# Input projections of linear attention and recurrence: from full-precision products to three rounded passes, with ScalarE and GpSimd splitting the weights

## What is computed

```
proj = h @ w_in                      # attention: 1024 x 3088, q, k, v, g, a_lr
log_a = log_sigmoid(a_lr @ w_gate_up + b_gate) / 16
...
proj = h @ w_in                      # recurrence: 1024 x 2048
gate_br, xb = split(proj)
xc = causal depthwise conv(xb)       # 4 taps
r, i = sigmoid(xc @ w_r + b_r), sigmoid(xc @ w_i + b_i)
h = modulate(rmsnorm(x, gain), shift, scale)     # ahead of both
```

## Time and profile before

| | us |
|---|---|
| median of 3 runs | 1944.4 (1943.58 to 1946.43) |
| the profiled execution | 1949.44 |
| its span | 1947.6 |
| TensorE busy in it | 1828.3 (94%) |
| VectorE, ScalarE busy | 1056.6, 733.3 |
| mean granted TensorE clock | 0.966 of 2.4 GHz |
| attention's input, first low-rank product to the end of slot 11 | 34.7 to 155 |
| recurrence's input, first product to the end of slot 7 | 600.6 to 676.6 |

### The profile page before, as it was taken

How to read it: one execution, slowest core, us unless ns; L and a number is a source line. 1 busy time by engine, 2 the same in 40 slices (tenths; PEclk the granted TensorE clock), 3 DMA queues, 4 the chain that set the end, 5 groups by cost and what they waited for, 6 DMA issues and landing times.

```text
span 1947.6 us, 22802 instructions
## 1 busy us (share of the span) xinstructions
PE 1828.3 (94%) x9181; PEld 1409.1 (72%) x9181; DVE 1056.6 (54%) x1561; ACT 733.3 (38%) x944; POOL 0.2 (0%) x4
## 2 busy tenths in 40 slices
PE   6999999999998989999999989998798899989998
PEld 3786677767777756777677756766445767779998
DVE  1332644447884336544478744037923663438886
ACT  3212433334662415322446640126624333034443
POOL 0000000000000000000000000000000000000000
PEclk9999899998999998999999989999899999989999
DMA  9847666687984696577868902335422222345550
GB/s 360 266 136 260 236 238 259 260 324 259 365 319 136 198 320 258 197 277 285 333 244 333 341 22 87 108 109 194 130 65 65 87 87 87 110 148 176 193 174 23
DMA packets 178593, 392.92 MB, mean 202 GB/s; under 512 B 11317, under 2 KB 102056, under 8 KB 162104
## 3 DMA queue, kind: packets, MB, share of 16 engines
q1 hardware_dynamic: 176814, 389.58, 56.4%
q10 hardware_dynamic: 1674, 1.88, 0.3%
HBM read 390.39 MB, written 1.05 MB: 201 GB/s over the span
## 4 chain that ended last, share of the span: by engine, by line
PE 85%; DVE 8%; ACT 3%; DMA 2%; issue 1%; SPq 0%; DVEq 0%; ACTq 0%
PE bank L493 20%; PE bank L767 18%; PE bank L795 9%; PE bank L1193 7%; PE bank L503 4%; PE bank L598 4%; PE bank L1204 3%; PE bank L779 3%; PE bank L558 3%; DVE work L1728 2%; DMA ring<-in_ada_w_dram 2%; PE bank L1149 2%; PE bank L810 1%; PE bank L515 1%; DVE parts L1978 1%
## 5 line engine op out<-in xcount | busy, mean ns | idle before, releaser
L1978 DVE TENSOR_TENSOR parts<-ring,parts 128x2048 fp32r<-128x2048 f32 x144 | 329.1, 2290 | 168.4 <-ACT parts L1424 167.4
L767 PE MATMUL bank<-parts 128*128 128x512 f32 x1536 | 369.1, 399 | 8.0 <-issue 4.7
L493 PE MATMUL bank<-hh,ring 128*128 128x256 f32 (+1 forms) x1408 | 369.5, 422 | 6.1 <-ACT hh L1329 3.7
L1424 ACT ACTIVATE parts<-ring 128x2048 fp32r<-128x2048 f32 x144 | 275.2, 1917 | 228.6 <-PE bank L767 162.3
L767 PEld LDWEIGHTS bank<-parts 128*128 128x128 f32 x1536 | 292.5, 192 | 77.7 <-issue 17.0
L493 PEld LDWEIGHTS bank<-hh,ring 128*128 128x128 f32 x1408 | 268.6, 192 | 106.4 <-issue 76.4
L1286 ACT ACTIVATE work<-bank 128x256 f32<-128x256 f32 (+3 forms) x223 | 98.3, 445 | 518.2 <-PE bank L493 254.1
L795 PE MATMUL bank<-parts 128*128 128x512 f32 x768 | 179.4, 391 | 3.7 <-DVE parts L2003 3.7
L795 PEld LDWEIGHTS bank<-parts 128*128 128x128 f32 x768 | 143.4, 188 | 36.7 <-DVE parts L2003 4.1
L1193 PE MATMUL bank<-parts 128*128 128x256 f32 x1056 | 131.1, 287 | 7.6 <-DVE parts L2481 7.6
L1193 PEld LDWEIGHTS bank<-parts 128*128 128x128 f32 x1056 | 130.1, 196 | 8.4 <-DVE parts L2481 8.4
(11 more groups left out here) (273 smaller groups left out, 1779.9 us busy)
## 6 DMA issues: line engine op xcount, KB each, us to landing
ring<-in_moe_w_gate_dram SPq DMA_DIRECT2D x64, 1024.0 KB, 6.5
ring<-in_moe_w_up_dram SPq DMA_DIRECT2D x64, 1024.0 KB, 7.4
ring<-in_moe_w_down_dram SPq DMA_DIRECT2D x64, 1024.0 KB, 6.8
ring<-in_ada_w_dram SPq DMA_DIRECT2D x48, 1024.0 KB, 7.3
ring<-in_w_in_dram SPq DMA_DIRECT2D x32, 1024.0 KB, 5.9
ring<-in_w_mod_dram SPq DMA_DIRECT2D x24, 1024.0 KB, 5.7
ring<-in_w_up_dram SPq DMA_DIRECT2D x22, 1024.0 KB, 5.1
ring<-in_gla_w_in_dram SPq DMA_DIRECT2D x12, 1024.0 KB, 7.7
```

Of the source, the lines that this page charges most:

```text
L493: ins = pe.matmul(ps[:, 0:n], w[:, k, m * P:(m + 1) * P], rhs(k), start=k == 0, stop=k == kt - 1)
L767: ins = pe.matmul(bank[:, :], xg[:, a_, k, tile * P:(tile + 1) * P], w[b_][:, j, :], start=k == 0 and n == 0, stop=k == KT - 1 and n == 2)
L1424: act.activation(moe_w[:, n % 3, 0, :], ring[:, g % RING, :], ACT.Identity)\
L1978: dve.tensor_tensor(moe_w[:, n % 3, 1, :], ring[:, (MOE_AT[layer] + AT[key]) % RING, :], moe_w[:, n % 3, 0, :].bitcast(F32), sub).then_inc ...
```

## The change

- A new list `SPLIT` holds the 20 projection slots. `linear` and `by_token` become `split_linear` and `split_by_token` there: three passes of float32r, with each half slot waited for on its own (`half_low`). The low-rank product gets three passes too.
- ScalarE writes the input with its shift, rounded, to a new buffer (`round_in`), and VectorE computes the low part in place of the unrounded input (`low_in`). `h_ready` is counted by VectorE, not ScalarE.
- ScalarE rounds each projection slot in two halves of 128 x 1024 (`high_halves`) into four buffers; the half of slot n waits for the landing of that slot and for TensorE's use of slot n-2. Its places among the drains are written out.
- GpSimd gets a program: 40 subtractions that leave the low half in the ring slot itself.
- The token inputs `x_in` and `c_in` land in the space of `g_s`.

```diff
+    SPLIT = [g for g, (what, _) in enumerate(SLOTS) if what in ("gla_in", "lru_in")]
...
+            def split_linear(to, h_of, first=False):
+                n = SPLIT_NTH[slot[0]]
+                slot[0] += 1
+                for m in range(2):
+                    pe.wait_ge(sem("half_low"), 2 * n + m + 1)
+                    w = halves_of(n, m)
+                    ps = to.fill(pe)
+                    for k in range(KT):
+                        if first and m == 0:
+                            fresh()
+                        for i, (a_, b_) in enumerate(PASSES):
+                            ins = pe.matmul(ps[:, 0:T], w[a_][:, k, :], h_of(b_, k), start=k == 0 and i == 0,
+                                            stop=k == KT - 1 and i == 2)
+                    close(to, ins)
+                    high_used[n, m] = (to.ready, to.n)
+                free_slot(to.ready, to.n)
...
+                        if t == 0 and k % 4 == 0:
+                            pe.wait_ge(sem("half_low"), 2 * n + k // 4 + 1)
...
-            pe.wait_ge(sem("low_rank_w"), 16)
+            pe.wait_ge(sem("low_rank_parts"), 1)
...
-                ins = pe.matmul(ps[0:16, 0:T], w_lr[:, k, :], h(k), start=k == 0, stop=k == KT - 1)
+                for i, (a_, b_) in enumerate(PASSES):
+                    ins = pe.matmul(ps[0:16, 0:T], low_rank_parts[:, a_, k, :], gla_parts(b_, k),
+                                    start=k == 0 and i == 0, stop=k == KT - 1 and i == 2)
...
-                linear("lru_in", to_act, h, T, first=j == 0)
+                split_linear(to_act, lru_parts, first=j == 0)
...
+            def round_in(dst, shift):
+                for k in range(KT):
+                    act.wait_ge(sem("h_scaled"), c(sem("h_scaled")))
+                    act.activation(dst[:, k, :], hh[:, k, T:TC], ACT.Identity, bias=shift[:, k:k + 1])\
+                        .then_inc(sem("h_rounded"), 1)
+            def high_halves(n):
+                g = SPLIT[n]
+                act.wait_ge(landed[g % RING], 16 * (g // RING + 1))
+                for b in range(2):
+                    if n >= 2 and SLOTS[SPLIT[n - 2]][0] == SLOTS[g][0]:
+                        act.wait_ge(*high_used[n - 2, b])
+                    act.activation(high_half(n, b), ring_half(n, b), ACT.Identity).then_inc(sem("half_high"), 1)
...
-            shift_in(mods[:, 0, 0:8])
+            act.wait_ge(sem("low_rank_w"), 16)
+            act.activation(low_rank_parts[:, 0], w_lr[:, :, :], ACT.Identity).then_inc(sem("low_rank_high"), 1)
+            round_in(gla_h, mods[:, 0, 0:8])
+            high_halves(0)
             take(g_lr[0:16, :], parts=16)
+            high_halves(1)
             for j in range(2):
                 take(g_q[:, j, :], scale=float(P) ** -0.5)
+            high_halves(2)
             take_mod()
...
             for j in range(2, 4):
                 take(g_q[:, j, :], scale=float(P) ** -0.5)
+            high_halves(3)
             take_mod()
             for j in range(4):
                 take(g_k[:, j, :], done=j == 3 or None)
+                if j % 2:
+                    high_halves(4 + j // 2)
             act.wait_ge(sem("gla_rest"), 1)
...
                 for t in range(TT):
                     take(g_v[:, t, j * 256:(j + 1) * 256])
+                high_halves(6 + j)
                 if j < 2:
                     take_mod()
...
-            shift_in(mods[:, 1, 0:8])
+            round_in(lru_h, mods[:, 1, 0:8])
+            high_halves(12)
+            high_halves(13)
...
                 take(l_xb[:, j, 3:3 + T])
+                if j % 2:
+                    high_halves(14 + j // 2)
                 if j in (3, 7):
                     take_mod()
...
+        @block.gpsimd
+        def _(pool):
+            for n in range(len(SPLIT)):
+                for b in range(2):
+                    pool.wait_ge(sem("half_high"), 2 * n + b + 1)
+                    pool.tensor_tensor(ring_half(n, b, of=ring_low), ring_half(n, b), high_half(n, b).bitcast(F32),
+                                       ALU.subtract).then_inc(sem("half_low"), 1)
...
+            def low_in(high, shift, before):
+                for k in range(KT):
+                    dve.wait_ge(sem("h_rounded"), before + k + 1)
+                    dve.scalar_tensor_tensor(out=hh_low[:, k, T:TC], in0=hh[:, k, T:TC], scalar=shift[:, k:k + 1],
+                                             in1=high[:, k, :].bitcast(F32), op0=add, op1=sub)\
+                        .then_inc(sem("h_ready"), 1)
...
+            dve.wait_ge(sem("low_rank_high"), 1)
+            tt(low_rank_parts[:, 1], w_lr[:, :, :], low_rank_parts[:, 0].bitcast(F32), sub, done=sem("low_rank_parts"))
             norm(gains[:, 0, :])
+            low_in(gla_h, mods[:, 0, 0:8], 0)
```

More of the change, by code:

```diff
@@ L243, in build @@
     MOE_AT = [next(i for i, (what, arg) in enumerate(SLOTS) if what == "moe" and arg[0] == layer) for layer in range(2)]
-    freed = {}
+    SPLIT = [g for g, (what, _) in enumerate(SLOTS) if what in ("gla_in", "lru_in")]
+    SPLIT_NTH = {g: n for n, g in enumerate(SPLIT)}
+    BY_TOKEN = SPLIT[4:8]
+    freed, high_used = {}, {}
     with ExitStack() as ctx:
@@ L255, in sem @@
             return sems[name]
+        with nc.sbuf_tensor("ring_low", [P, RING, SLOT], F32R) as ring_low:
+            pass
         ring = sb("ring", [P, RING, SLOT])
@@ L261, in build @@
         x = sb("x", [P, KT, T])
+        with nc.sbuf_tensor("hh_low", [P, KT, TC], F32R) as hh_low:
+            pass
         hh = sb("hh", [P, KT, TC])
@@ L298, in build, with room @@
             he_t = parts[:, at:at + 4 * D_EXPERT].rearrange("p (i o n) -> p i o n", i=2, o=2)
+        with nc.sbuf_tensor("work_rounded", [P, ROOM], F32R) as work_rounded:
+            pass
         work = sb("work", [P, ROOM])
         used = [0, 0]
-        def room(*shape):
+        def room(*shape, of=None):
             n = int(np.prod(shape))
-            a = work[:, used[0]:used[0] + n]
+            a = (work if of is None else of)[:, used[0]:used[0] + n]
             used[0] += n
@@ L346, in build @@
         g_gam = room(4, CHUNKS)
+        x_in, c_in = [g_s[:, 2 * i:2 * i + 2].rearrange("p n h v -> p n (h v)") for i in range(2)]
+        gla_high, gla_h = room(4, D, of=work_rounded), room(KT, T, of=work_rounded)
+        low_rank_parts = room(2, KT, 16, of=work_rounded)
         assert used[0] <= rows_from
@@ L459, in build, with ring_half, high_half, halves_of @@
         PARAMS_FROM, PARAMS_EACH = 9, 3
+        def ring_half(n, b, of=ring):
+            g = SPLIT[n]
+            w = of[:, g % RING, :].rearrange("p (k n) -> p k n", k=KT)
+            return w[:, 4 * b:4 * b + 4, :] if g in BY_TOKEN else w[:, :, b * P:(b + 1) * P]
+        def high_half(n, b):
+            tile = (gla_high if SLOTS[SPLIT[n]][0] == "gla_in" else lru_high)[:, 2 * (n % 2) + b, :]
+            return tile.rearrange("p (k n) -> p k n", k=4 if SPLIT[n] in BY_TOKEN else KT)
+        def halves_of(n, b):
+            return high_half(n, b), ring_half(n, b, of=ring_low)
         block = ctx.enter_context(nc.Block())
@@ L504, in by_token, with split_by_token @@
                     close(to, ins)
+                free_slot(to.ready, to.n)
[14 more added lines that the diff above has]
+                    high_used[n, m] = (to.ready, to.n)
+                free_slot(to.ready, to.n)
+            def split_by_token(to, h_of):
+                n = SPLIT_NTH[slot[0]]
+                slot[0] += 1
+                for t in range(TT):
+                    ps = to.fill(pe)
+                    for k in range(KT):
+                        if t == 0 and k % 4 == 0:
+                            pe.wait_ge(sem("half_low"), 2 * n + k // 4 + 1)
+                        w = halves_of(n, k // 4)
+                        for i, (a_, b_) in enumerate(PASSES):
+                            ins = pe.matmul(ps[:, 0:256], h_of(b_, k)[:, t * P:(t + 1) * P], w[a_][:, k % 4, :],
+                                            start=k == 0 and i == 0, stop=k == KT - 1 and i == 2)
+                    close(to, ins)
+                high_used[n, 0] = high_used[n, 1] = (to.ready, to.n)
                 free_slot(to.ready, to.n)
@@ L601, in residual_out @@
                 free_slot(to_dve.ready, to_dve.n)
-            pe.wait_ge(sem("low_rank_w"), 16)
+            pe.wait_ge(sem("low_rank_parts"), 1)
             ps = to_act.fill(pe)
+            low = lambda k: hh_low[:, k, T:TC]
+            gla_parts = lambda o, k: low(k) if o else gla_h[:, k, :]
             for k in range(KT):
                 fresh()
-                ins = pe.matmul(ps[0:16, 0:T], w_lr[:, k, :], h(k), start=k == 0, stop=k == KT - 1)
+                for i, (a_, b_) in enumerate(PASSES):
+                    ins = pe.matmul(ps[0:16, 0:T], low_rank_parts[:, a_, k, :], gla_parts(b_, k),
+                                    start=k == 0 and i == 0, stop=k == KT - 1 and i == 2)
             close(to_act, ins)
             low_rank = to_act.n
```

(4 more changed lines are left out.)

36 lines of the change are left out of this document (23 added, 13 removed).

## The result

The changed kernel takes 1951.0 us (median of 7 runs, 1948.99 to 1955.92), the kernel before 1945.6 beside it (7 runs, 1940.03 to 1946.43): ratio 1.0036, 95% interval 1.0022 to 1.0049. By the medians it is 5.4 us slower (by the ratio 7.0 us); 11.3 us faster was forecast. The profiled execution's span went from 1947.6 to 1952.8 us.

A forecast was written before the change was run, and what follows sets the result against it. TensorE, busy 94% of the span, was taken as the bound. Linear attention -11.7, recurrence -1.2 and both engines at once +1.6 gave -11.3 us, from 1944.4 to 1933.1 us; own range 1930 to 1939, 8 in 10 from 1930 to 1957.

The forecast's parts named there:

- (1): Projection slots in both stages: 48 passes of 0.120 us, 5.76 us in place of 6.91, saving 23.0 us.
- (2): Linear attention's input: low parts queued behind VectorE's norm end the low-rank product at about 41.0 us, +1.0 us.
- (3): Attention's first half slot: ScalarE rounds, GpSimd subtracts in 2.3 us; slot 0 starts 0.2 us later still.
- rival A: Slower case, chance 0.34: GpSimd and VectorE instructions exclude each other, delaying context and gates; total +8.0, 1952.4 us.
- (4): Supply between slots: GpSimd needs 4.6 us a slot, TensorE 5.76; costs arise only above 2.9 us a half.
- (5): ScalarE's queue: rounding waits for slot landings and delays drains, +0.9 us in the attention, +0.8 in the recurrence.
- (6): Recurrence's start: TensorE starts 6.2 us later, behind norm, rounding and GpSimd's low part, plus 1.0 us for the clock.
- (7): VectorE beside GpSimd: two-input instructions take double time, about four low parts at the start, +1.6 us; elsewhere slack.
- the clock's term: Recurrence's start: 1.0 us added for a lower granted clock after TensorE's longer idle time of 9.9 us.
- the row of loads: Modulation chunks ending both projections, paced by the ring's DMA: loads move with TensorE, so gains ahead of them are kept.
- (8): The two inputs land elsewhere in the work buffer: no instruction or wait comes with that, so nothing.

The follow-up runs named there:

- eight pieces: Each GpSimd subtraction of the changed kernel cut into eight of 128x128, same result; ratio 1.0005 to the kernel before.

## Why the prediction was wrong

**(1) The passes: right.** The 48 passes of the first slot take from 42.45 to 48.4 us, 5.9 us, and 5.65 to 5.8 later on, 0.118 to 0.120 us each, wherever TensorE had not stopped before.

**(2), (3) The first slot:** it begins 8.7 us after the norm's first instruction; before it was 6.4, so +2.3 where +1.2 was forecast. GpSimd's size was right, 2.35 us a half for the 2.3 taken. Of the 1.1 us that were missing, 0.6 is contention: in the kernel whose GpSimd only writes, the slot begins at +8.1 and TensorE doesn't wait for GpSimd. The contention has a form that neither case had: VectorE's eight low parts stand back to back and took their usual 3.25 us, and GpSimd's first half was the one that waited, 3.81 us long instead of 2.35. The other 0.5 is the low-rank product, which ended at 41.8 us and not at 41.0; TensorE had stood for 4.8 us ahead of it (1.9 before), and the granted clock from 37.5 to 42.4 us was 0.69 (0.87 before). Rival A had the low parts wait, +3.8 here and +3.6 in the recurrence. Neither came, and without them its +8.0 would be +0.6; that it lies near the measured +5.4 is in part luck, since it held nothing for the slow stretches behind the stops.

**(4) Steady supply: right.** 4.7 us a slot against 5.8; in the attention's later slots TensorE doesn't wait for GpSimd once. With eight pieces, at 6.7 to 7.9 us, it did, as the step said. (The share named for rival A was too high: 40 halves of 2.3 us are 92 us, under half of the two stages, not 80%.)

**(5) Landing waits: the mechanism right, the sizes too large.** ScalarE stood for landings five times in the attention, 17.7 us in all and up to 6.1 at the third slot, and TensorE's waits for ScalarE at line 634 rose from 0.8 to 1.5 us in the attention (+0.9 forecast) and from 0.2 to 0.5 in the recurrence (+0.8).

**(6) The recurrence's start:** TensorE's first pass came 8.7 us after the norm's first instruction in place of 1.2, so +7.5 where +6.2 was forecast; on VectorE, without contention, +6.4. The +1.0 for the clock did not come. The granted clock of the first 10 us was indeed lower, 0.77 where the kernel before had 0.83, but the first 48 passes took 7.68 us, 1.9 more than their 5.76, and the first 64 records of before took 15.66 us, 1.8 more than their 13.8:

```profile
606.00:616.00 10.00, 9.62 (x65) 9.62 (x66) 9.14 (x17) 2.33 (x5) 7.67 (x5) 0.77 0.06 8
```

**(7) Both engines at once: this step failed.** It held the term at 1.6 us, as VectorE at half speed for four instructions, "elsewhere VectorE has slack". The engines don't share, they take turns by whole instructions, and a held scan of 0.30 us took 2.33. The slack was read from a mean (39 of 124 us busy) over a stage in which VectorE has one stretch with a follower: the scans and 4 subtractions, then the decay on ScalarE and the turned context on TensorE. That stretch grew from 7 us (5.17 + 1.80) to 19.3, which used up its 4 us of slack; in the recurrence the small instructions ahead of the convolution and the convolution itself have such a follower in the gates. TensorE lost 8.3 us there and 5.4 at the gates, 13.7 together, 3.9 in the slow stretches behind these two stops, which no step held, and 2.4 more than forecast at the two starts. Less the 1.6 that the step held, the 0.9 by which the clock's term and the 0.7 by which the landing waits were too large, that is 16.8 us, where forecast and result are 16.7 apart by the medians and 15.9 by the stages; one profile differs from the next by as much. Steps (1) to (6) gave 11.7 and 1.2 us, and the two kernels without the exclusion gave 11.9 and -0.6 (writes only), 10.3 and 1.0 (on VectorE). The -0.6 shows a weak point of another sentence, that a gain made ahead of the row of loads is kept: with writes only the recurrence's last slot ends 1.3 us earlier against the norm than before, but TensorE's waits for the loads behind it rose from 5.5 to 8.8 us.

The Trainium skill, page "SBUF — State Buffer", section "Who interferes with whom", has this as a rule, with blocking for the whole instruction, and for a VectorE instruction with two inputs none by a GpSimd instruction that only writes. The runs bear out both parts: a held scan took 2.33 us beside halves of 2.35, and 16 scans took 5.17 us beside writes. The prediction cited it, priced the context at 9 us and the gates at 4.5, which came out at 8.3 and 5.4, and wrote of rival A that it decides the sign once a half takes over about 2 us, while it took a half at 2.3. The choice of the forecast over rival A (0.45 to 0.34) rested on the mean busy share alone.

**(8) Buffers:** nothing seen.

## What to carry to other kernels

Where GpSimd is given work beside VectorE, look for VectorE's runs of many short instructions that somebody waits for, and price each at one whole GpSimd instruction, not at a share of time; a mean busy share says nothing on it. Short GpSimd instructions make the price small (of the four lengths here 256 columns, 0.70 us, was best), and moving only the few colliding ones to VectorE frees that stretch too (the attention at 131.2 us). Here all of the work on VectorE was better than either, ratio 0.9940. Count a stop of TensorE at more than its length: 5.4 us cost another 2.5 at granted clock 0.76. A first product that waits for a chain of norm, rounding and subtraction can begin with the passes that need only the first link, if its weights have landed.

## What was unexpected of the hardware

Who waits depends on how the work stands (seen in the traces, not varied by a run of its own): in a back-to-back run of eight two-input instructions VectorE let GpSimd wait for 1.5 us, while among instructions that wait for each other it alternated with GpSimd one to one. And beside GpSimd's writes alone, two-input instructions ran free, but one-input `tensor_scalar` from SBUF to SBUF was still held: two of 8 columns took 1.30 us together where before they took 0.38, and the eight two-input ones behind them took 1.57 us, as before. In that kernel's timeline of the recurrence:

```profile
594.27 1.30 DVE L1836 TENSOR_SCALAR misc<-cols 128x8 f32<-128x8 f32 x2
...
598.51 1.57 DVE L1841 SCALAR_TENSOR_TENSOR misc<-misc 128x8 f32<-128x8 f32 x8
```
